# Neighbourhood attention in a two-block kernel: who splits the weights, a new table of projection pieces, v on other banks, layer norm sums by TensorE

## The reference, cut to what matters

```
h = rms_norm(x, norm1_g);  z = h @ w_in                # 2560 columns: a, gate, q, k, v (512 each)
u = a * sigmoid(gate)
y = depthwise_conv(u, 31 taps) + dw_bias               # over positions, 512 channels
conv_out = silu(layer_norm(y, ln_g, ln_b))             # over channels
q, k = rms_norm per head (8 heads of 64)
attn_out = for each head: softmax(q k / 8 + rpb) v     # each token sees an 8 x 16 window of a 16 x 64 grid
x = x + concat(conv_out, attn_out) @ w_out             # then a gated MLP, then the second block
```

## Time and profile before

| | us |
|---|---|
| median of 3 runs | 2753.36 (2751.15 to 2753.69) |
| the profiled execution's own time | 2753.43 |
| its span, first to last instruction | 2751.7 |

### The profile page before, as it was taken

The page is one execution under the profiler, slowest core; times in us unless marked ns, Lnnn a source line. Parts: engine busy times, 40 slices in busy tenths (PEclk is TensorE's granted clock), DMA queues, the critical chain, the costliest instruction groups (busy, mean ns, idle before and its releaser), DMA issues.

```text
span 2751.7 us, 27584 instructions
## 1 busy us (share of the span) xinstructions
PE 2503.4 (91%) x11028; PEld 1959.8 (71%) x11028; DVE 1235.3 (45%) x1206; ACT 674.1 (24%) x919; POOL 936.1 (34%) x431
## 2 busy tenths in 40 slices
PE   8978867899999999998988988795999999999979
PEld 6756545778888888887765554484888888888857
DVE  7977774242222222226635546548322222222465
ACT  3135445120000000102045556603111000110231
POOL 4422110434444443434411111044443343343353
PEclk9988988999999999999989988798999999999989
DMA  3210101211111111112100000120111111111112
GB/s 127 48 38 23 31 1 44 79 45 48 46 54 46 46 49 50 46 50 89 56 23 16 16 16 0 60 63 16 54 46 54 46 46 53 46 46 53 53 32 84
DMA packets 47791, 126.41 MB, mean 46 GB/s; under 512 B 19104, under 2 KB 19104, under 8 KB 45664
## 3 DMA queue, kind: packets, MB, share of 16 engines
q1 hardware_dynamic: 40592, 124.90, 14.7%
q10 hardware_dynamic: 7120, 0.40, 0.2%
HBM read 116.68 MB, written 8.79 MB: 46 GB/s over the span
## 4 chain that ended last, share of the span: by engine, by line
PE 67%; DVE 7%; issue 6%; ACT 5%; POOL 2%; DMA 1%; SPq 0%; POOLq 0%; DVEq 0%; ACTq 0%
PE ps L476 59%; PE ps L866 3%; DMA weight_raw<-w_out 1%; PE ps L798 1%; ACT sb_e L1266 1%; ACT sb_e L1264 1%; DVE conv_out L1479 1%; POOL branch_out L435 1%; POOL weight_hi L396 1%; ACT sb_e L1268 1%; DVE sb_softplus_lo L1803 1%; POOL weight_lo L398 1%; DVE residual L1910 1%; PE ps L841 1%; DVE sb_weights L1818 1%
## 5 line engine op out<-in xcount | busy, mean ns | idle before, releaser
L396 POOL TENSOR_TENSOR weight_hi<-weight_raw,zero_col 128x1024 fp32r<-128x1024 f32 (+1 forms) x195 | 376.5, 1931 | 1754.9 <-PE ps L476 1401.4
L476 PE MATMUL ps<-input_hi,weight_hi 128*128 128x512 f32 x1904 | 608.4, 401 | 69.9 <-DVE input_lo L1445 34.8
L476 PE MATMUL ps<-input_lo,weight_hi 128*128 128x512 f32 x2032 | 641.0, 397 | 19.2 <-DVE gate_lo L1914 17.4
L476 PE MATMUL ps<-input_hi,weight_lo 128*128 128x512 f32 x1904 | 594.8, 394 | 0.0
L398 POOL TENSOR_TENSOR weight_lo<-weight_raw,weight_hi 128x1024 fp32r<-128x1024 f32 (+1 forms) x195 | 505.0, 2590 | 15.3
L476 PEld LDWEIGHTS ps<-input_hi,weight_hi 128*128 128x128 f32 x1904 | 358.5, 192 | 159.9 <-issue 66.4
L476 PEld LDWEIGHTS ps<-input_lo,weight_hi 128*128 128x128 f32 x2032 | 389.9, 192 | 105.5 <-ACT input_lo L972 13.9
L476 PEld LDWEIGHTS ps<-input_hi,weight_lo 128*128 128x128 f32 x1904 | 363.6, 191 | 77.8
L476 PE MATMUL ps<-hidden_hi,weight_hi 128*128 128x512 f32 x864 | 231.4, 390 | 3.4 <-DVE hidden_lo L1677 3.4
L476 PE MATMUL ps<-hidden_hi,weight_lo 128*128 128x512 f32 x864 | 231.8, 390 | 0.0
L476 PE MATMUL ps<-hidden_lo,weight_hi 128*128 128x512 f32 x864 | 231.4, 390 | 0.0
(11 more groups left out here) (239 smaller groups left out, 2643.6 us busy)
## 6 DMA issues: line engine op xcount, KB each, us to landing
weight_raw<-w_ff SPq DMA_DIRECT2D x40, 512.0 KB, 3.5
weight_raw<-w_mlp SPq DMA_DIRECT2D x32, 512.0 KB, 3.6
weight_raw<-w_mlpd SPq DMA_DIRECT2D x32, 512.0 KB, 3.6
weight_raw<-w_ffd SPq DMA_DIRECT2D x20, 512.0 KB, 3.5
weight_raw<-w_out SPq DMA_DIRECT2D x16, 512.0 KB, 3.6
weight_raw<-w_in SPq DMA_DIRECT2D x16, 512.0 KB, 3.6
residual<-x SPq DMA_DIRECT2D x7, 1024.0 KB, 8.9
weight_raw<-w_qkv SPq DMA_DIRECT2D x12, 512.0 KB, 3.7
```

The lines of the kernel that those rows point to most:

```text
L396: pool_.tensor_tensor(WH[:, slot, 0:width], raw, ZERO[:].to_broadcast([P, width]), ALU.add).then_inc(s["w_hi"], 1)
L476: last = mm(PS[:, b + 2 * c + h, :], w[:, slot, k * n + P * c:k * n + P * (c + 1)], a[:, k, h * H2:(h + 1) * H2], start=(k == first and st ...
```

## The change

- **Splits.** Units 2 to 21 are split by ScalarE (`weight_hi`) and VectorE (`weight_lo`), written out in their queues; of unit 1 ScalarE makes `WH` and GpSimd `WL`. GpSimd goes on with unit 22. Unit 2's `weight_hi` stands behind the guess for the first norm's factor (which needs the mean of squares that TensorE takes just ahead of unit 2), its `weight_lo` behind VectorE's refinement of that factor.
- **Start of the attention.** The first v unit (unit 10) goes to banks 6 and 7. The means of squares of q and k stand at chunk 5 and 6 of the next unit, before at chunk 3. Pieces 0 to 3 of pair 0 are issued ahead of the first `scores`, and turn 0 has none.
- **The table.** Pieces per turn are 4, 4, 4, 4, 2, 2, 3, 1 (before 5, 5, 5, 2, 2, 2, 2, 1). In turn 7 `scores(n + 1)` stands behind the last v piece. The transposes of v are spread over turns 0 and 1.
- **VectorE's order.** Taps are spread anew and end in pair 2 (31 beside GLU, 10 ahead of turn 0, 28 a pair); copies out of PSUM stand at other places.
- **Layer norm.** TensorE sums the four blocks itself (`ln_sums`: 8 matmuls in place of 2, twice), ScalarE squares and makes the first guess within turns 2 and 3, VectorE's adds are gone, and its last steps are in turn 5. The `hi` parts of three of w_out's inputs move from ScalarE to VectorE.
- **Loads.** SP loads all 8 w_out units without a wait for x; x is reloaded from ScalarE's queue after `mix_lo`.

```diff
-BESIDE = (((0, 1), (2,), (3,), (4,)),
-          ((5,), (6,), (7,), (8, 9)),
-          ((10,), (11,), (12,), (13, 14, "m0")),
-          ((15,), (), (16,), ("m1",)),
-          ((17,), (18,), (), ("m2",)),
-          ((19,), (20,), (), ("m3",)),
-          ((21,), (22,), (), ()),
-          ((23,), (), (), ()))
-TAPS_AT = (5, 4, 5, 2, 3, 3, 1, 3)
+BESIDE = (((0, 1), (2,), (), (3,)),
+          ((4,), (5,), (6,), (7,)),
+          ((), (8, 9), (10,), ("m0", 11)),
+          ((12,), (13,), (14,), (15, "m1")),
+          ((), (16, 17), (), ("m2",)),
+          ((18,), (19,), (), ("m3",)),
+          ((20,), (21,), (), (22,)),
+          ((), (23,), (), ()))
...
@@ SP
-            for j in range(2):
-                load_unit(U_OUT + j, j % 2, w_out[j])
-            sp.wait_ge(s["mix_lo"], 8)
-            for k in range(4):
-                sp.dma_start(X[:, 2 * k:2 * k + 2, :], x[:, 2 * k:2 * k + 2, :]).then_inc(s[f"x_in{k}"], 16)
-            for j in range(2, 8):
+            for j in range(8):
                 load_unit(U_OUT + j, j % 2, w_out[j])
@@ GpSimd
-            splits(4, U_TAIL + 2 * TAIL - 4)
+            splits(U_OUT + 2, U_TAIL + 2 * TAIL - U_OUT - 2)
@@ TensorE
-            pe.wait_ge(s["bank_free"], U_QKV + 1)
-            unit(U_QKV + 2, 0, 0, k_ready=k_means)
+            pe.wait_ge(s["bank_free"], U_QKV)
+            unit(U_QKV + 2, 0, 6, k_ready=k_means)
+            def ln_sums(t, signal):
+                for h in range(2):
+                    for m in range(4):
+                        last = mm(PS[:, h, :], MEAN[:], t(m)[:, h * H2:(h + 1) * H2], start=(m == 0), stop=(m == 3))
+                last.then_inc(s[signal], 1)
+            for what in BESIDE[0][0] + BESIDE[0][1] + BESIDE[0][3]:
+                next_piece(0, what)
             scores(0)
...
                     turn(n, 0)
-                    if n < 4 * CBLOCKS - 1:
+                    if j < CBLOCKS - 1:
+                        scores(n + 1)
+                    if j == 1:
+                        v_turn(c, 1)
+                    slot(0)
+                    turn(n, 1)
+                    slot(1)
+                    if j == CBLOCKS - 1 and c < 3:
                         scores(n + 1)
                     if j == 0:
                         v_turn(c, 0)
@@ ScalarE
+            def weight_hi(u):
+                act.wait_ge(s[f"w_loaded{u % 2}"], 16 * (u // 2 + 1))
+                if u >= 2:
+                    act.wait_ge(s["unit_done"], u - 1)
+                copy(WH[:, u % 2, :], RAW[:, u % 2, :]).then_inc(s["w_hi"], 1)
...
             first_guess(bank(6), RS[:], "mean_done", 1, "ln_exp")
+            weight_hi(2)
@@ VectorE
             scale_from(1)
+            def weight_lo(u):
+                dve.wait_ge(s["w_hi"], u + 1)
+                tt(WL[:, u % 2, :], RAW[:, u % 2, :], WH[:, u % 2, :].bitcast(f32), ALU.subtract)\
+                    .then_inc(s["w_split"], 1)
+            weight_lo(2)
...
+            def first_part(c, j):
+                if j == 0 and c:
+                    weight_lo(U_QKV + 3 * c + 4)
+                elif j == 1:
+                    conv(1)
+                elif j == 2:
+                    evac(c + 1, 0, 0)
+                elif j == 3:
+                    head_norm(4 * c + 4, 5)
+                elif j == 4:
+                    evac(c + 1, 1, 0)
+                elif j == 5:
+                    weight_lo(U_QKV + 3 * c + 6)
+                    head_norm(4 * c + 6, 5)
+                elif j == 6:
+                    head_norm(4 * c + 7, 5)
+                elif j == 7:
+                    head_lo(c + 1, 1)
+            def second_part(c, j):
+                if j == 2:
+                    weight_lo(U_QKV + 3 * c + 5)
+                elif j == 4:
+                    head_norm(4 * c + 5, 5)
+                elif j == 6:
+                    head_lo(c + 1, 0)
+                elif j == 7:
+                    evac(c + 1, 2, 0)
+                conv(min((4, 4, 3, 3, 2, 3, 3, 4)[j], 4 * TAPS - tap[0]))
```

More of the change, by code:

```diff
@@ L407, in _ @@
             pool.wait_ge(s["w_split"], 1)
[L408 to L409 removed]
+            pool.wait_ge(s["w_hi"], 2)
+            pool_.tensor_tensor(WL[:, 1, :], RAW[:, 1, :], WH[:, 1, :].bitcast(f32), ALU.subtract)\
+                .then_inc(s["w_split"], 1)
             pool.wait_ge(s["scale_ready"], 1)
@@ L1181, in _ @@
             mix_hi(7, OC[3][:])
+            act.wait_ge(s["mix_lo"], 8)
+            for k in range(4):
+                act.dma_start(X[:, 2 * k:2 * k + 2, :], x[:, 2 * k:2 * k + 2, :]).then_inc(s[f"x_in{k}"], 16)
             for k in range(KD):
@@ L1494, in _ @@
                 if c:
-                    conv(4 if c == 3 else 6)
+                    weight_lo(2 * c + 2)
+                    conv(6)
                 dve.wait_ge(s["unit_done"], 2 * c + 2)
@@ L1500, in _ @@
                 chain(tt(UP[:, c, PADT:PADT + T], TC[:], TB[:], ALU.mult))
+                weight_lo(2 * c + 3)
                 if c:
-                    conv(2 if c == 3 else 6)
+                    conv(3 if c == 3 else 5)
             MIX = [Y[:, c, :] for c in range(4)] + [OC[c][:] for c in range(4)]
@@ L1563, in _ @@
             head_lo(0, 1)
-            evac(0, 2, 0)
+            evac(0, 2, 6)
+            weight_lo(U_QKV + 4)
             scores_in(0, 0)
@@ L1569, in _, with last_pair @@
             probs(0, 1)
+            conv(2)
+            def first_part(c, j):
+                if j == 0 and c:
+                    weight_lo(U_QKV + 3 * c + 4)
+                elif j == 1:
+                    conv(1)
+                elif j == 2:
+                    evac(c + 1, 0, 0)
+                elif j == 3:
+                    head_norm(4 * c + 4, 5)
[9 more added lines that the diff above has]
+            def second_part(c, j):
+                if j == 2:
+                    weight_lo(U_QKV + 3 * c + 5)
+                elif j == 4:
+                    head_norm(4 * c + 5, 5)
+                elif j == 6:
+                    head_lo(c + 1, 0)
+                elif j == 7:
+                    evac(c + 1, 2, 0)
+                conv(min((4, 4, 3, 3, 2, 3, 3, 4)[j], 4 * TAPS - tap[0]))
+            def last_pair(j):
+                if j == 0:
+                    weight_lo(U_OUT + 1)
+                    conv(4 * TAPS - tap[0])
+                elif j == 1:
+                    dve.wait_ge(s["ln_mean"], 1)
+                    for m in range(4):
+                        stt(Y[:, m, :], bank(0), -2.0, Y[:, m, :], ALU.mult, ALU.add).then_inc(s["ln_cent"], 1)
+                elif j in (2, 3, 4):
+                    k = MIX_ORDER[j - 2]
+                    if j == 2:
+                        dve.wait_ge(s["unit_done"], U_OUT)
+                    dve_.tensor_copy(INH[:, k, :], MIX[k]).then_inc(s["mix_hi"], 1)
+                    mix_lo(k, MIX[k], 0, j - 2)
+                elif j == 5:
+                    dve.wait_ge(s["ln_y0"], 2)
+                    chain(stt(bank(0), bank(0), EPS / 2.0, TB[:], ALU.add, ALU.mult))
+                    chain.wait()
+                    chain(stt(bank(0), bank(0), -1.5, TA[:], ALU.add, ALU.mult))
+                    chain.wait()
+                    for m in range(4):
+                        tt(Y[:, m, :], bank(0), Y[:, m, :], ALU.mult).then_inc(s["ln_norm"], 1)
             for c in range(4):
@@ L1572, in _ @@
                     n = CBLOCKS * c + j
-                    taps_left = TAPS_AT[j] if c < 3 else 0
                     more = n < 4 * CBLOCKS - 1
-                    if more:
+                    if more and j < CBLOCKS - 1:
                         scores_in(n + 1, 0)
                         scores_in(n + 1, 1)
-                    if taps_left:
-                        conv(1)
-                        taps_left -= 1
+                    if c < 3:
+                        first_part(c, j)
+                    if more and j == CBLOCKS - 1:
+                        scores_in(n + 1, 0)
+                        scores_in(n + 1, 1)
+                    if c < 3:
+                        conv(min(1, 4 * TAPS - tap[0]) if j == CBLOCKS - 1 else 0)
                     if more:
@@ L1633, in _ @@
+                        second_part(c, j)
+                    else:
+                        last_pair(j)
             for m in range(4):
```

156 lines of the change are left out of this document (55 added, 101 removed).

## The result

| | before | after |
|---|---|---|
| median, us | 2752.55 (2746.34 to 2755.49, 20 runs) | 2756.44 (2753.97 to 2758.46, 20 runs) |
| ratio of the runs | | 1.0017 (95% interval 1.001 to 1.0024) |
| profiled execution, its span | 2753.43, 2751.7 | 2754.87, 2753.2 |

The account below looks back on a forecast made before the run. TensorE bounded no pair by itself: it waits and returns at the lower clock level. Terms +1.3 - 6 + 1.6 - 4 - 2 - 5.5 = -14.6 from 2753.43 gave 2739 us, range 2720 to 2754.

Parts of the forecast that it names:

- Start: In GLU, a new wait and clock loss at unit 2, less a gain at unit 1: 6.4 us later.
- the signs that I named: Trace marks of the forecast, such as unit 2 about 5.7 us late, turn 0 near 159, unit 22's wait near 3.
- GLU to first turn: Behind GLU, unit 9's means no longer wait: 5.1 us won, so turn 0 stands 1.3 us later.
- Pairs 0 to 2: First three attention pairs would take 69, 75.4 and 75.4 us: 6 won, 1.6 lost, 4 won.
- the walk: Turn-by-turn comparison of TensorE's and VectorE's work in a pair: 71.4 us at the upper clock level, 14 of waits.
- Pair 3: Last attention pair, with layer norm: 11.6 us won from turn 24 to 25, most given back; 2 won.
- Into w_out: At w_out, the wait for unit 22 falls from 7.79 to 3.0 us, with 0.7 of clock: 5.5 won.
- C: Attention: each of five waits a pair brings TensorE back at 1.2 GHz, so slower, 2769 us; chance 0.11.
- A: Attention pairs lose no clock and layer norm runs at full level: 2724 us; chance 0.28.
- B: Attention turns are bound by VectorE, delays are not made up, a pair takes 80: 2753 us, no change; chance 0.14.
- D: In GLU, unit 2 does not wait, ScalarE and VectorE having unseen slack: 2731 us; chance 0.05.
- the rule weighed in the prediction: VectorE and GpSimd lock shared SBUF ports for whole instructions; by it alone, three pairs would be up to 24 us lower.

Follow-up runs that it names:

- the block in lots: The kernel after, with ScalarE's 55 bias-table DMAs issued in five lots of 11 instead of one block: 2732.8 us against 2753.7, ratio 0.9926.
- Alone, the part: The kernel before, with only the w_out loads issued without waiting and x reloaded from ScalarE's queue: 2748.0 us against 2753.7, ratio 0.9979.
- the block of 27: The kernel after, with the 55 bias-table DMAs in lots of 11, 27, 11 and 6, the 27 between units 5 and 6: 2736.6 us, ratio 0.9944.

## Why the prediction was wrong

The forecast failed in one step, a term that *Start* put at nothing: "From unit 3 on, a unit has 10.9 us on PE, and ScalarE's 1.1 and VectorE's 1.23 lie inside." I compared durations and not what is queued ahead of them. ScalarE's queue holds 38.2 us of DMA issues between units 5 and 6; the row of it was in the trace of before, and I left it unread because the engine is idle by the page's count. The kernel with the block in lots measured 2732.8 (0.9926), 6 us better than my 2739. That is nearer, but not the forecast come true: in the profile after the start brought 2.1 more than I said and the pairs 5.9 more, and pair 3 brought 2.7 less. Of the signs that I named, only turn 0 (159 said, 176.59 measured) pointed at the stretch that failed.

The other steps, one by one, by the table of places above:

- *Start.* Unit 2 waited 5.83, 5.7 forecast. Unit 1 was better: the mean began at 33.35, 3.2 earlier than the earlier trace rows, not 1.1. The earlier `weight_lo` is 1.2 of that (unit 1's first matmul at 12.50, before 13.74). I had nothing for the clock: TensorE came to the upper level at 13.4 instead of 18.5, worth the other 1.9. Its timeline there, before and then after:

```profile
18.17 0.82 PE L476 MATMUL ps<-input_hi,weight_lo 128*128 128x512 f32 x2
...
13.38 0.63 PE L473 MATMUL ps<-input_lo,weight_hi 128*128 128x512 f32 x2
```

- *GLU to first turn.* Forecast 5.1 won behind GLU; between unit 2 and turn 0 the kernel lost 16.0, and the block alone took 19.2. With the block in lots the stretch from unit 2 to turn 0 took 114.5, before 119.5: 5.0 won, though the slow matmuls behind unit 2's wait are in it. Unit 9's means came without a wait, as said.
- *Pairs 0 to 2.* Forecast: 69, 75.4 and 75.4; measured 68.7, 72.8 and 72.3. Gained 14.3, forecast 8.4. What was too big are the waits. Pair 1 before, then pairs 1 and 2 after (columns as in the earlier trace rows):

```profile
233.00:306.70 73.70, 62.63 (x342) 44.34 (x340) 55.71 (x91) 37.19 (x84) 14.64 (x6) 0.93 0.11 28
...
245.30:318.10 72.80, 61.35 (x341) 43.67 (x341) 61.88 (x97) 40.52 (x88) 0.00 (x0) 0.95 0.11 29
318.10:390.40 72.30, 61.96 (x346) 44.09 (x344) 61.23 (x97) 40.44 (x88) 0.00 (x0) 0.95 0.09 26
```

  TensorE was busy 61.4 and 62.0 us, which is my 57 and 4 for the clock, and it was idle for 11.4 and 10.3, where I had 14. Turn 2's wait was 1.99, but turn 4's 0.42 to 0.50; I had 2.1 for each. (The turns of the walk add up to 71.3, not 71.4.)
- *Pair 3.* Forecast 2 won; 0.7 lost. From turn 24 to 25 it took 17.2, not 13.5: I forgot the 2.90 us for the copy of v. The sum itself took 8.7 of the 9 said. From turn 25 to w_out 8.5 was given back, 9.8 forecast, with waits of 5.68 and 5.41 for `probs_t`.
- *Into w_out.* Wait of 3.19, 3.0 forecast; of the 5.5 only 3.0 are seen between w_out's first matmul (460.36 before, 465.27 after) and unit 22, as w_out began with slow matmuls for 5 us. Alone, the part brought 5.7.

Rivals: C did not happen, and A did not either: the clock granted in the three pairs was 0.90, 0.95 and 0.95, before 0.89, 0.93 and 0.94. Nor did B; D is excluded. The slower end that I gave a chance of 0.11 came by another mechanism, one I had not listed. As for the rule weighed in the prediction: the two taps of the earlier trace rows grew by 3.3 us beside a subtraction of GpSimd, but over the three pairs twelve splits by GpSimd cost the taps 5 to 6 us in all, so the measured mean was the better guide for the sum.

## What to carry to other kernels

When work with a due time moves to another engine, list that engine's whole queue around the new place, DMA issues included: they are not in its busy time. Lay the due times against the issue times; as long as the stock ahead covers a block it costs nothing, and then each microsecond counts. A step moved to another engine is only won as far as it was bare before: of VectorE's adds about a third was hidden, of TensorE's sums nothing.

## What the runs showed of the hardware

Issuing a small DRAM-to-DRAM DMA took 0.69 us each from ScalarE's queue (55 in 38.2, 27 in 18.69), and ScalarE began no other instruction meanwhile; from GpSimd's queue 0.63 (55 in 34.64). Behind one and the same wait of 5.83 us TensorE's matmuls stayed at the lower clock level for 2.7 us in the kernels after and with lots, and for 6.1 us with the block of 27: the same code, 1.7 us apart.
